# Prompt attention of a decoder trunk: another order of its first loads, three waits split, one table load and two sorts moved

## The reference, cut to what matters

```python
oa, _ = banded_attn(qa, ka, va, 0, A_WINDOW, w['a_sink'])   # 4 q heads, 2 kv heads, look back <= 128
ob = dilated_prompt(qb, kb, vb)                             # 6 heads; (128,1), (512,4), (2048,16)
# in both, for a block of 128 queries:
s = jnp.einsum(...) * (hd ** -0.5)
s = jnp.where(mask, s, -jnp.inf)
p = jnp.exp(s - m)                 # m: row maximum, with the sink in group A
o = einsum(p, v) / (p.sum() + exp(sink - m))
```

## Time and profile before

| | us |
|---|---|
| median of 3 runs | 3264.35 (3263.09 to 3264.71) |
| the profiled execution, device time | 3269.89 |
| its span, first to last instruction | 3268.1 |
| PE busy in the span | 3056.9 (94%) |
| DVE, ACT, POOL busy | 1571.2 (48%), 817.4 (25%), 350.9 (11%) |
| granted TensorE clock, mean | 0.966 |
| prompt attention: first load issued, last matmuls of its tiles | 588.7, about 865 |

### The profile page before, as it was taken

One profiled execution on the slowest core, in us unless ns is written; L12 is line 12 of the kernel. 1 busy time (PEld: TensorE's weight loads), 2 busy tenths in 40 slices (PEclk: granted clock), 3 DMA queues, 4 the chain that ended last, 5 costly groups with the idle time before them and its releaser, 6 DMA issues. The chain is left out here.

```text
span 3268.1 us, 65648 instructions
## 1 busy us (share of the span) xinstructions
PE 3056.9 (94%) x27080; PEld 2594.3 (79%) x27080; DVE 1571.2 (48%) x3052; ACT 817.4 (25%) x1506; POOL 350.9 (11%) x473
## 2 busy tenths in 40 slices
PE   7999999799788898885997999999999999999998
PEld 7999998466477777784785888888888998888887
DVE  6211121577565666654334444444446445444545
ACT  5000000465423233322233211122113221122112
POOL 4000000454233223310000000000000000000000
PEclk9999999899899999996998999999999999999999
DMA  4122121523222230002455310111114201110111
GB/s 152 70 73 70 69 85 48 152 83 102 72 88 83 96 107 25 22 13 73 147 177 170 125 49 28 51 51 51 51 48 156 89 26 51 51 51 26 51 45 66
DMA packets 144827, 248.84 MB, mean 76 GB/s; under 512 B 21536, under 2 KB 100896, under 8 KB 144096
## 3 DMA queue, kind: packets, MB, share of 16 engines
q1 hardware_dynamic: 144608, 245.68, 22.5%
HBM read 185.12 MB, written 60.52 MB: 75 GB/s over the span
## 5 line engine op out<-in xcount | busy, mean ns | idle before, releaser
L2757 DVE TENSOR_TENSOR m_y<-m_y,m_db 128x512 f32<-128x512 f32 x512 | 351.3, 687 | 323.4 <-PE m_db L2526 323.1
L2524 PE MATMUL m_ub<-m_hh,m_wuh 128*128 128x352 f32 (+1 forms) x1280 | 452.4, 353 | 17.5 <-DVE m_hl L2703 17.4
L2525 PE MATMUL m_ub<-m_hl,m_wuh 128*128 128x352 f32 (+1 forms) x1280 | 450.6, 352 | 0.0
L2526 PE MATMUL m_ub<-m_hh,m_wul 128*128 128x352 f32 (+1 forms) x1280 | 450.0, 352 | 0.0
L2524 PE MATMUL m_db<-m_wdh,m_uh 128*128 128x512 f32 x1024 | 406.8, 397 | 4.8 <-DVE m_wdl L2712 4.7
L2526 PE MATMUL m_db<-m_wdh,m_ul 128*128 128x512 f32 x1024 | 403.8, 394 | 0.0
L2525 PE MATMUL m_db<-m_wdl,m_uh 128*128 128x512 f32 x1024 | 402.6, 393 | 0.0
L183 PE MATMUL p_bank<-p_xh,p_wh 128*128 128x416 f32 x800 | 286.4, 358 | 11.6 <-DVE p_wl L304 11.6
L184 PE MATMUL p_bank<-p_xl,p_wh 128*128 128x416 f32 x800 | 284.0, 355 | 0.0
L185 PE MATMUL p_bank<-p_xh,p_wl 128*128 128x416 f32 x800 | 283.0, 354 | 0.0
L2524 PEld LDWEIGHTS m_ub<-m_hh,m_wuh 128*128 128x128 f32 x1280 | 241.4, 189 | 46.0 <-issue 12.5
(11 more groups left out here) (393 smaller groups left out, 5022.0 us busy)
## 6 DMA issues: line engine op xcount, KB each, us to landing
m_wur<-w_up SPq DMA_DIRECT2D x64, 512.0 KB, 6.0
m_wdr<-w_dn SPq DMA_DIRECT2D x64, 512.0 KB, 4.1
p_ring<-units SPq DMA_DIRECT2D x30, 768.0 KB, 6.1
out_projT<-p_ob SPq DMA_DIRECT2D x100, 208.0 KB, 1.9
cp_z<-out_projT SPq DMA_DIRECT2D x8, 1408.0 KB, 7.9
p_wr<-w_fm SPq DMA_DIRECT2D x20, 512.0 KB, 3.6
p_mix<-mixT SPq DMA_DIRECT2D x16, 512.0 KB, 5.0
p_x<-x SPq DMA_DIRECT2D x16, 512.0 KB, 3.6
```

Source lines behind the costliest of these rows:

```text
L2524: pe.matmul(out, wh, mh, start=first, stop=False)
L2525: pe.matmul(out, wh, ml, start=False, stop=False)
L2526: return pe.matmul(out, wl, mh, start=False, stop=last)
L2757: dve.tensor_tensor(yh, yh, db[(2 * a + h) % ND][:, :], ALU.add).then_inc(y_added, 1)
```

## The change

- SP's order for pair 0: behind the constants one more quarter of q, then v, then the rest of k, then the last two quarters of q.
- The masks of the far keys leave this place. They are issued at the top of turn u = 1 of SP's loop, so behind the stores of pair 0 and ahead of the loads of pair 2 (q, k, v and the strided v).
- The identity gets a semaphore of its own, `ident_in`. PE waits for it at its first turning, Pool before its first diagonal; `consts_in` counts three loads, and only DVE waits for it.
- ACT waits for `ones_set` and takes one exponential of a column of ones (128x1), before its first wait for data.
- Pool sorts two quarters of pair 0 at first, the third after the diagonals of tile 1, the fourth after those of tile 3.

```diff
             sp.dma_start(mw[:, 0, CK:CK + 2 * P], mask_w[:, 0, CK:CK + 2 * P]).then_inc(consts_in, 16)
-            sp.dma_start(idt[:, :], ident).then_inc(consts_in, 16)
-            for c in range(1, NCL):
+            sp.dma_start(idt[:, :], ident).then_inc(ident_in, 16)
+            load_q(0, 1)
+            load_v(0)
+            load_k(0)
+            for c in range(2, NCL):
                 load_q(0, c)
-            load_k(0)
-            load_v(0)
-            sp.dma_start(mw[:, 0, 0:CK], mask_w[:, 0, 0:CK]).then_inc(mask_in, 16)
-            for r in range(1, NCL):
-                sp.dma_start(mw[:, r, :], mask_w[:, r, :]).then_inc(mask_in, 16)
             for u in range(PAIRS):
+                if u == 1:
+                    sp.dma_start(mw[:, 0, 0:CK], mask_w[:, 0, 0:CK]).then_inc(mask_in, 16)
+                    for r in range(1, NCL):
+                        sp.dma_start(mw[:, r, :], mask_w[:, r, :]).then_inc(mask_in, 16)
...
-            for c in range(NCL):
+            for c in range(2):
                 sort(0, c)
-            pool.wait_ge(consts_in, 64)
+            pool.wait_ge(ident_in, 16)
...
                     fill(2 * m + h)
+                if m in (1, 3):
+                    sort(0, 2 + m // 2)
...
+                if at == 0:
+                    pe.wait_ge(ident_in, 16)
...
-            pe.wait_ge(consts_in, 64)
...
-            act.wait_ge(consts_in, 64)
+            act.wait_ge(ones_set, 1)
+            act.activation(warm[:, :], onesb[:, 0:1], ACT.Exp)
...
-            dve.wait_ge(consts_in, 64)
+            dve.wait_ge(consts_in, 48)
```

More of the change, by code:

```diff
@@ L447, in prompt_attention @@
         rec = s.sb("p2_rec", [P, 8])
+        warm = s.sb("p2_warm", [P, 1])
         NSB = 4
@@ L453, in prompt_attention @@
         consts_in = s.sem("p2_consts_in")
+        ident_in = s.sem("p2_ident_in")
         mask_in = s.sem("p2_mask_in")
```

## The result

| | before | after |
|---|---|---|
| median of 19 runs each, us | 3266.27 (3261.67 to 3281.29) | 3273.82 (3264.44 to 3285.49) |
| profiled execution, its span, us | 3269.89, 3268.1 | 3272.3, 3270.5 |
| granted clock, mean | 0.966 | 0.965 |

The change makes the kernel slower: ratio 1.0023 (95%: 1.0013 to 1.0032), which is +7.5 us (4.2 to 10.4). The forecast was -0.7 us. The 19 runs of before contain the three on which the forecast stood; those lie in the lower half of their spread.

A forecast was written before the change was run, and what follows sets the result against it. PE was taken to bound later prompt attention, with the loss at its start. Start -2.4 plus pair 2 +1.7 made -0.7 us, from 3264.35 to 3263.6 us; 8-in-10 range 3260.6 to 3267.0.

The forecast's parts named there:

- the start's gain that goes on: Start of prompt attention: of 2.6 us gained at tile 4's scores, 2.4 us (1.2 to 3.6) carries on.
- displacement of PE at tile 22: Pair 2: PE stands 1.7 us (1.0 to 4.0) because Pool's diagonals wait behind its sort of late k.
- the clock behind it: TensorE's clock after the tile 22 stall: no cost in the sum; a fall appeared only in a rival.
- the same 3.3 us give 606.2 now: Start: clock rises 3.3 us after PE goes on, at 606.2, so tile 5 and part of tile 6 cost as before.
- Start of the chain: Stage start: DVE's earlier start and the early table load bring the first exponential 2.6 us earlier, to 595.1.
- v and k: Pair 0's loads: PE waits 0.6 us for v; k lands at 602.9, starting tile 4's scores 2.6 us earlier.
- Pool's third sort: Pool between pair 0's diagonals: third quarter of q lands about 603.7, leaving 1.4 us of slack, so no cost.
- Masks ahead of pair 2: Far masks queued before pair 2's loads: k 3.1 us late, less 1.4 us of slack, a 1.7 us PE stall.
- if q, now in the middle, runs at 380: Pair 2's loads: q at 380 GB/s gives back 1.2 us, making k's delay 2.4 us, its lower bound.
- 3.3 us at any rate seen here: Argument against the rival of a whole gain: the masks' 1.44 MB need 3.3 us at any rate seen.
- slower than before: Rival, chance 0.15: tile 22's stall outweighs the start, +2.8 us, or +3.8 us if the clock falls.
- Scores of tile 26 within 2 us of 653.2: Sign at pair 2: the prediction is wrong if tile 26's scores don't start within 2 us of 653.2.

The follow-up runs named there:

- e10: Kernel before with only the new order of pair 0's loads and Pool's sorts between diagonals, old waits, far masks behind these loads: ratio 0.9995, stage 284.37 us.
- e12: Kernel before, unaltered, timed and traced as if it were new: ratio 0.9986 (3265.08 against 3269.52 us), stage 287.49 us.
- e2: Kernel before with only the four far masks moved ahead of pair 2's loads: ratio 1.0026, stage 292.07 us.
- e4: Changed kernel unaltered, timed again with a second trace: ratio 1.0026 against before, stage 291.23 us.
- e6: Kernel before, loads untouched, with six unused Pool multiplications after its first sort of pair 2's k: ratio 1.0013, stage 292.06 us.
- e11: Changed kernel unaltered, timed once more with a third trace: ratio 1.0014 against before, stage 289.92 us.
- e13: Changed kernel unaltered, a trace only: stage 290.13 us, PE's wait at tile 22 2.5 us.
- e14: Changed kernel unaltered, another trace only: stage 291.84 us, PE's wait at tile 22 3.07 us.
- e15: Changed kernel unaltered, a further trace only: stage 290.84 us, PE's wait at tile 22 2.65 us.
- e7: Kernel before with two small identity loads, each waited for by SP, at the stage's end: ratio 1.0004, next stage 3.8 us later (291.51).
- e3: Changed kernel with the far masks issued behind pair 2's loads instead of ahead of them: ratio 1.0002 against before, stage 286.60 us.
- e9: Kernel before with only the split waits and the early exponential, order of loads and sorts as before: ratio 1.0000, stage 287.78 us.
- e1: Changed kernel with the far masks issued at the start again, behind pair 0's loads: ratio 1.0001 against before, stage 286.61 us.
- e5: Changed kernel with Pool's sorts of pair 2 put behind later diagonals, SP's queue untouched: ratio 1.0004 against before, stage 287.17 us.

## Why the prediction was wrong, step by step

The forecast named the two places, the path and the engines of each. The sign is wrong because its two effects were to cancel within a microsecond, and three terms beside or inside them were off, all in one direction:

| us, earlier is minus | forecast | profiled pair | six traces of the change, two of before |
|---|---|---|---|
| the start's gain that goes on | -2.4 | -1.2 | -1.1 |
| displacement of PE at tile 22 | +1.7 | +2.5 | +2.7 |
| the clock behind it | 0 | +0.7 | +1.4 |
| sum, up to tile 28 | -0.7 | +2.0 | +3.0 |

**The steps that failed** are two: "the same 3.3 us give 606.2 now", from which the 2.4 us come, and the clock behind the stall, which was put at nothing. The stall itself had the right path and was mis-sized. No single term decides the sign in the profiled pair: corrected alone, they give +0.5, +0.1 and 0.0.

**Start of the chain: right.** The first exponential 2.40 us earlier (2.6 forecast): 595.26 in before's times, against 595.1. DVE's first work at 594.14 (593.8). The turning of tile 1 ends at 598.89 (598.9). The drain of about 1.38 us behind a table load that the Trainium skill states ("ScalarE: Activation LUTs", What ACT_TABLE_LOAD costs) doesn't show in after either: the exponential of one column starts 1.30 us after the load does (591.23 against 589.93).

**v and k: right at tile 4, wrong in what is carried on.** v was in before it was asked for (a wait of 0.6 was forecast) and k landed so that tile 4 starts at 602.53 in before's times, 2.99 us earlier (2.6, 1.2 to 3.3). Then "the same 3.3 us give 606.2 now, so that tile 5 and part of tile 6 are paid as before" failed. Two things are wrong in it. It took the clock to be low until 3.3 us after PE had gone on, as in before; here it had risen at about 600, fell in the wait for k, and came back 6.3 us after PE went on (603.76 to 610.04). In the other five traces it had not risen at all before tile 4, and it rose 3.3 to 5.1 us after tile 4 began. And it took 2.93 us as the price of a slow tile, which was a tile that had met the rise; a tile that is slow throughout takes 3.56 (603.76 to 607.32). So 1.16 us are left at tile 6 instead of the 2.4 forecast, outside of even that term's own 1.2 to 3.6 by a little. The other traces agree: tile 4 is 2.0 us earlier in the mean of the six, tile 6 1.1. e10 is the counter-example: same start of tile 4 as in the profiled run, a pause of 0.31 us ahead of it, and 21.72 - 17.74 = 4.0 us gained at tile 6, in one trace.

**Pool's third sort: right.** It started at 605.22, 604.0 in before's times, against 603.7 forecast, and PE met no wait at tile 2 or 3.

**Masks ahead of pair 2: mechanism right, size low.** Pool's sort of k came at 63.85 instead of 61.12 us from the first load, while the tiles around it ran 1.19 earlier: 3.9 us late against the rest of the program, 3.1 forecast (2.4 to 5.4). The stall was 2.33 us here and 2.33 to 3.07 in all traces that have it, against 1.7 (1.0 to 4.0); the slack is 3.9 - 2.3 = 1.6 (1.4 forecast). The delay of 3.1 us was chosen between the 3.7 us of the masks at 394 GB/s and the 2.4 that are left "if q, now in the middle, runs at 380"; the lower bound pulled it down. (The forecast's "3.3 us at any rate seen here" is below what its rows give: the highest rate in them, 394 GB/s, makes 3.7.) The Trainium skill ("DMA: Bandwidth & Descriptors", Queues, rings and completion order) says that each DMA engine takes its descriptors in ring order, and the trace agrees: k landed at 63.79 instead of 61.07 us from the first load, 3.9 us late against the tiles around it, which is the whole of the masks (3.7) and a little more. `spread_rec` of tile 22 is displaced by 1.32 + 1.19 = 2.5.

**The clock behind the stall: left out of the sum.** The forecast had it in the rival "slower than before", with the argument that the gap at 601.5 to 604.5 "was at the slow clock anyway, so the trace doesn't say that such a gap lowers it". That is true of that one gap. But the same trace shows such gaps at the full clock in other stages, and there the clock falls. One of the first is in `project`: PE stands 2.94 us until 40.59, and of the two stretches below, the pause still has the full clock and the one behind it half.

```profile
40.59 1.27 PE L193 MATMUL p_sum<-p_rs,p_ones 128*128 128x416 f32 x2 [2.94 <-POOL p_part L382]
```

```profile
37.60:40.60 3.00, 0.07 (x2) 0.01 (x1) 3.00 (x2) 0.00 (x0) 2.85 (x2) 1.00 0.83 253
41.10:44.40 3.30, 3.30 (x8) 2.17 (x7) 2.44 (x5) 2.68 (x6) 0.00 (x0) 0.50 0.74 252
```

Of the nine PE gaps of 2.2 to 3.2 us in before's trace that begin at the full clock, eight have the clock fall within them or in the 2 us behind them; in e12, the same kernel, it is five of nine. So a fall was to be expected more often than not, and to be priced. At tile 22 it came every time: in all eight traces with a stall of 2.3 to 3.1 us (after, e2, e4, e6, e11, e13, e14, e15) the clock is at half in its end or behind it, for 3.4 us in seven of them and for 6.8 in e14. In after this costs 0.68 us net: 5.84 us from `spread_rec` of tile 22 to tile 28 against 5.16, although a wait of 0.80 us for DVE (657.89 in before) is gone. The mean of the six traces is 6.50, so 1.35 us.

**The rival that came nearest** is "slower than before", with a chance of 0.15: the stall outweighs the start, and the clock falls. It gave +2.8 for the two terms at their bounds (1.2 gained, 4.0 lost) and +3.8 with the clock's 1.0; the six traces have 1.1, 2.7 and 1.4, together +3.0. So the mechanism was on the list, and its chance was too small.

**The rest of the measured loss stays open.** The runs give +7.5 (4.2 to 10.4), and the two repeats 0.26% and 0.14%, with medians 4.2 us apart both times; the stage accounts for 3.0, at most 4.2. The three medians of the change agree (3273.82, 3273.27, 3273.72), while those of before lie between 3265.08 and 3270.42 in its six groups, so part of the 7.5 us may be where before's own median happened to fall. Behind it the traces show nothing: from the next stage's first matmul to the end, the six traces of the change need 2390.7 us in the mean (2386.9 to 2396.1), the other twelve 2390.7 (2382.1 to 2396.8). A later start of the next stages alone costs its own length (e7). e12 shows that one program can differ by 4.4 us from itself in just such a comparison, which is of the size of the remainder, but four of the comparisons with the masks ahead of k lie above 1 (1.0023, 1.0026, 1.0026, 1.0014), so chance is not shown to be the answer either. With a scatter of some 15 us behind the stage, the difference of these two means is uncertain by about 4 us, so a term of a few us there could not be seen in this many traces.

**The range.** Measured from its base, 3260.6 to 3267.0 is -3.8 to +2.7 us: the profiled pair's +2.0 lies inside, the six traces' +3.0 just above. It held the terms of the change and nothing of the scatter of a median. The three runs of before gave 3264.35; all 19 gave 3266.27, and later groups 3265.08 to 3270.42. The base alone moved by up to 6 us, about as much as the whole range is wide. And 0.94 for "the same" gave too little to a loss at just over 0.2%.

**The signs that the forecast had named.** Wait for k at tile 4 about 2 us and under 4: 3.05 (2.38 to 4.02 in the other traces). Pool 3 to 5 us: 4.45. First wait of PE on a diagonal, 1 to 4 us: 2.33. Scores of tile 26 within 2 us of 653.2: 655.23 in before's times, 2.03 off, the one that told of the error. Later stages of the same length: yes, as far as traces tell.

## What to carry to other kernels

A load that is moved is paid by what stands behind it in the queue, and the one who pays may be two engines away: ask which in-order engine waits for the next load, what else stands behind its wait, and how much slack that has (here 1.6 us). A load that is wanted late goes behind the urgent ones, not ahead of them: the same masks behind pair 2's loads cost nothing (e3). A chain that is started earlier is worth nothing if it ends in a wait (e9); where PE pauses in it, price the tiles behind the pause at the slow clock's full price (3.56 us here), not at that of a tile that met the rise. And before a term of the clock is put at nothing, look for pauses of the same length in the other stages of the same trace: they were there.

## What the runs showed of the hardware that was not expected

- The granted clock was down to half behind every PE wait of 2.3 to 3.1 us at tile 22, where it had been full for some 40 us; a wait of 0.8 us (657.89 in before) left it at full. In the other stages it fell at most, not all, of such pauses: 8 of 9 of 2.2 to 3.2 us in before, 5 of 9 in e12. One of them, 2.24 us long at the same place of the program, is followed by a fall in before (1192.41 to 1194.65) and not in e12 (1182.11 to 1184.35).
- It can rise for the wrong 3 us: in after from 599.80 to 603.21, of which PE was idle for most. Three of the nine traces with this start show it (after, e1, e5), so the same program pays it in one execution and not in the next.
- SP's issue is held behind the load of v: the two loads of k that follow it took 3.50 us to issue in after, against 1.11 in before, where the load behind v took 6.28.
- The same program's whole time lies between 3260 and 3277 us in 35 runs of one group, at a mean granted clock near 0.965. Comparisons of kernels that differ by less than 5 us need the stage's own length, read in several traces.
